# Gate logits of the linear attention: one stacked single-pass product instead of a float32 product

## What is computed

```python
IN_COLS = 2 * GLA_KW + 2 * GLA_VW + 2 * GATE_RANK + 3 * CONV_W     # GATE_RANK = 16, GLA_KW = 512
q, k, v, g, lf, lb, cb, cc, cx = split_proj(hx @ w_in[i])
la_f = heads(jax.nn.log_sigmoid((lf @ w_gf + b_gf).astype(jnp.float32)) / GATE_NORM, GLA_DK)
la_b = heads(jax.nn.log_sigmoid((lb @ w_gb + b_gb).astype(jnp.float32)) / GATE_NORM, GLA_DK)
```

## Time and profile before

| | |
|---|---|
| median of 3 runs | 2288.86 us (2288.14 to 2289.62) |
| span of the profiled execution | 2285.8 us |
| TensorE busy | 2266.4 us, 99% |
| TensorE weight loads busy | 1864.5 us, 82% |
| VectorE busy | 1556.3 us, 68% |
| ScalarE busy | 1109.7 us, 49% |
| GpSimd busy | 223.5 us, 10% |
| mean granted TensorE clock | 0.997 of 2.4 GHz |

### The profile page before, as it was taken

One profiled execution on the slowest core, in us unless ns is written; L12 is line 12 of the kernel. 1 busy time (PEld: TensorE's weight loads), 2 busy tenths in 40 slices (PEclk: granted clock), 3 DMA queues, 4 the chain that ended last, 5 costly groups with the idle time before them and its releaser, 6 DMA issues.

```text
span 2285.8 us, 28964 instructions
## 1 busy us (share of the span) xinstructions
PE 2266.4 (99%) x10345; PEld 1864.5 (82%) x10345; DVE 1556.3 (68%) x1869; ACT 1109.7 (49%) x1531; POOL 223.5 (10%) x361
## 2 busy tenths in 40 slices
PE   9999999999999999999999999999999999999998
PEld 7888888888888888888878877787888888888886
DVE  7886778778867877887767664556555545555556
ACT  6446455555545545545463463545444344444444
POOL 0121001111111111110011000000210011100110
PEclk9999999999999999999999999999999999999999
DMA  8983679978888888886677664564665666656663
GB/s 311 331 272 97 206 235 320 317 267 293 275 281 287 273 301 269 272 280 215 220 242 245 209 203 129 186 220 158 210 203 194 207 207 198 207 185 201 195 195 126
DMA packets 250005, 528.12 MB, mean 231 GB/s; under 512 B 22144, under 2 KB 22544, under 8 KB 248592
## 3 DMA queue, kind: packets, MB, share of 16 engines
q1 hardware_dynamic: 214256, 405.32, 54.2%
q0 software_dynamic: 33664, 116.17, 14.8%
q10 hardware_dynamic: 1952, 4.85, 0.6%
HBM read 517.87 MB, written 4.21 MB: 228 GB/s over the span
## 4 chain that ended last, share of the span: by engine, by line
PE 97%; DVE 1%; ACT 1%; DMA 0%; issue 0%; SPq 0%; ACTq 0%; DVEq 0%; POOLq 0%
PE acc L1798 30%; PE acc L1807 29%; PE acc L1802 29%; PE tp L1869 2%; PE m L1880 1%; PE acc L1820 0%; PE acc L1825 0%; PE acc L1830 0%; PE tp L2206 0%; PE tp L2224 0%; PE tp L2218 0%; PE acc L2000 0%; PE tp L2131 0%; PE acc L1853 0%; PE acc L1851 0%
## 5 line engine op out<-in xcount | busy, mean ns | idle before, releaser
L1090 DVE TENSOR_TENSOR wlo<-wring,whi 128x1024 fp32r<-128x1024 f32 x762 | 919.5, 1216 | 562.6 <-ACT whi L565 455.4
L565 ACT ACTIVATE whi<-wring 128x1024 fp32r<-128x1024 f32 (+1 forms) x510 | 532.1, 1047 | 720.4 <-PE acc L1807 719.3
L1798 PE MATMUL acc<-whi,xhi 128*128 128x512 f32 x2056 | 558.5, 393 | 0.1
L1802 PE MATMUL acc<-whi,xlo 128*128 128x512 f32 x2056 | 550.0, 389 | 0.0
L1807 PE MATMUL acc<-wlo,xhi 128*128 128x512 f32 x2056 | 549.9, 389 | 0.0
L1802 PEld LDWEIGHTS acc<-whi,xlo 128*128 128x128 f32 x2056 | 386.0, 188 | 81.1
L1807 PEld LDWEIGHTS acc<-wlo,xhi 128*128 128x128 f32 x2056 | 386.0, 188 | 80.7
L1798 PEld LDWEIGHTS acc<-whi,xhi 128*128 128x128 f32 x2056 | 381.2, 188 | 86.3 <-issue 9.0
L575 ACT ACTIVATE whi<-wring 128x1024 fp32r<-128x1024 f32 x266 | 280.8, 1059 | 319.8 <-PE acc L1807 318.1
L1120 DVE SCALAR_TENSOR_TENSOR macc<-mring,csil,macc 128x512 f32<-128x512 f32 x480 | 344.0, 747 | 29.3 <-DMA mring<-w_mod 23.0
L460 POOL DMA_DIRECT2D mring<-w_mod x192 | 138.9, 724 | 1047.4 <-DVE macc L1120 998.9
(11 more groups left out here) (277 smaller groups left out, 1313.7 us busy)
## 6 DMA issues: line engine op xcount, KB each, us to landing
wring<-w_up SPq DMA_DIRECT2D x216, 512.0 KB, 4.7
wring<-w_down SPq DMA_DIRECT2D x216, 512.0 KB, 5.1
mring<-w_mod POOLq DMA_DIRECT2D x192, 512.0 KB, 5.3
wring<-w_in SPq DMA_DIRECT2D x184, 512.0 KB, 5.2
wring<-w_gate SPq DMA_DIRECT2D x88, 512.0 KB, 4.3
wring<-w_out SPq DMA_DIRECT2D x64, 512.0 KB, 4.9
tmpT<-blk POOLq DMA_DIRECT2D x128, 32.0 KB, 3.4
gbig<-ctx_in POOLq DMA_DIRECT2D x2, 1024.0 KB, 8.1
```

Source lines behind the costliest of these rows:

```text
L565: act.activation(whi[:, piece_slot(c, piece), 0:half], wring[:, g4, piece * half:(piece + 1) * half], ACT.Copy).then_inc(hi_done, 1)
L1090: dve.tensor_tensor(wlo[:, h4, 0:half], wring[:, g4, piece * half:(piece + 1) * half], whi[:, h4, 0:half].bitcast(F32), ALU.subtract).then ...
L1798: pe.matmul(acc[:, 2 * pair + t, :], hi[:, tile, t * P:(t + 1) * P], whi[:, h4, w], start=(tile == starts), stop=False)
L1802: pe.matmul(acc[:, 2 * pair + t, :], lo[:, tile, t * P:(t + 1) * P], whi[:, h4, w], start=False, stop=False)
```

## The change

The gate product takes the same split into rounded value and remainder, but the parts stand below each other along the contraction, in one 128-row product of type float32r. Rows 0 to 31 of `lrankT` are the rounded rank values, rows 32 to 63 their remainders, rows 64 to 95 the rounded values again, and rows 96 to 127 ones. `wg` has the rounded gate matrix in the first two row groups and its remainder in the third; in row 96 the rounded bias, in row 97 its remainder, and zeros below.

To get the rank values three times, the rank block's weights are written three times side by side (`round_rank`, `remainder_rank`, 96 columns), so its product gives 96 rows. ScalarE copies all 96, and VectorE puts the remainder into rows 32 to 63 (`rank_split`). `wg` is put together once: GpSimd loads the matrix, the bias and zeros in ten DMAs into two scratch areas, `wg_raw` and `wg_rest`, ScalarE rounds `wg_raw` to `wg` and VectorE combines rows 64 to 127 with `wg_rest`. That is the new step `stack_gates`, at (cc0, 3) ahead of `z`, and the gate product waits for it (`wg_stacked`).

```diff
@@ -41,6 +41,7 @@
 RANK2 = 32
+RANK_ROWS = 3 * RANK2
 OFF_Q, OFF_K, OFF_V, OFF_G, OFF_L, OFF_CB, OFF_CC, OFF_CX = 0, 512, 1024, 2048, 3072, 3104, 4128, 5152
@@ -144,6 +145,7 @@
         ones = small[:, 14, 0:1]
+        gate_sign = small[:, 14, 1:2]
         blk = sb("blk", [P, T, NB])
@@ -183,15 +185,17 @@
             states = sb("states", [P, 2, GH, DV], scope=ph)
-            wg = sb("wg", [P, 2, GH * DK], scope=ph)
+            wg = sb("wg", [P, 2, GH * DK], F32R, scope=ph)
             gbig = sb("gbig", [P, 2 * D], scope=ph)
             gk = sb("gk", [P, T, GH * DK], scope=ph)
-            lrankT = sb("lrankT", [P, S], scope=ph)
+            lrankT = sb("lrankT", [P, S], F32R, scope=ph)
             epos = sb("epos", [P, 2, S], scope=ph)
             orstd = sb("orstd", [P, T, GH], scope=ph)
+        wg_raw = silg[:, 0, :].rearrange("p (d c) -> p d c", d=2)
+        wg_rest = silg[:, 1, :].rearrange("p (d c) -> p d c", d=2)
         u_g = gbig[:, :].rearrange("p (t d) -> p t d", t=T)
@@ -241,7 +245,8 @@
         ctx_in_s = sem("ctx_in_s")
-        wg_in = sem("wg_in")
+        wg_in, wg_rounded, wg_stacked, rank_split, sign_set = (
+            sem(n) for n in ("wg_in", "wg_rounded", "wg_stacked", "rank_split", "sign_set"))
         spill_s = sem("spill_s")
@@ -336,10 +341,10 @@
         BESIDE[1].update({
-            ("cc0", 3): (("z", 0, 0, 0),), ("cx0", 0): (("z", 0, 0, 1),),
+            ("cc0", 3): (("stack_gates", 0, 0, 0), ("z", 0, 0, 0)), ("cx0", 0): (("z", 0, 0, 1),),
             ("cx0", 1): (("z", 0, 1, 0),), ("cx0", 2): (("z", 0, 1, 1),),
             ("cx0", 3): (("suffix", 0, 0, 0), ("suffix", 0, 0, 1)), ("cb0", 0): (("suffix", 0, 1, 0), ("suffix", 0, 1, 1)),
             ("cb0", 1): (("ctx_state", 0, 0, 0),), ("cb0", 2): (("ctx_state", 0, 1, 0),),
@@ -370,6 +375,15 @@
         MOVES = 16 * 16
+        def rank_piece(slot, piece):
+            src = wring[:, slot, piece * 4 * RANK2:(piece + 1) * 4 * RANK2].rearrange("p (k n) -> p k n", k=4)
+            return src.unsqueeze(2).broadcast_to([P, 4, 3, RANK2])
+        def thrice(dst, slot):
+            return dst[:, slot, 0:4 * RANK_ROWS].rearrange("p (k c n) -> p k c n", k=4, c=3)
         block = ctx.enter_context(nc.Block())
@@ -518,9 +532,23 @@
             pool.wait_ge(h_added, H_MLP)
-            pool.memset(lrankT[RANK2:RANK2 + 1, :], 1.0).then_inc(pool_set, 1)
+            pool.wait_ge(pool_set, 1)
+            pool.memset(gate_sign[2 * RANK2:P, :], -1.0).then_inc(sign_set, 1)
+            pool.wait_ge(sign_set, 1)
+            pool.memset(gate_sign[RANK_ROWS:RANK_ROWS + 1, :], 1.0).then_inc(sign_set, 1)
+            pool.wait_ge(sign_set, 2)
+            pool.memset(lrankT[RANK_ROWS:P, :].bitcast(F32), 1.0).then_inc(pool_set, 1)
             pool.wait_ge(in_set, IN_SET[0]["v1"])
-            pool.dma_start(wg[:, :, :], gates_w).then_inc(wg_in, 16)
+            bias, zeros = gates_w[RANK2:RANK2 + 1], gates_w[RANK2 + 1:RANK2 + 31]
+            for copy in range(3):
+                pool.dma_start(wg_raw[RANK2 * copy:RANK2 * (copy + 1)], gates_w[0:RANK2]).then_inc(wg_in, 16)
+            for row in range(2):
+                pool.dma_start(wg_raw[RANK_ROWS + row:RANK_ROWS + row + 1], bias).then_inc(wg_in, 16)
+            pool.dma_start(wg_raw[RANK_ROWS + 2:P], zeros).then_inc(wg_in, 16)
+            pool.dma_start(wg_rest[2 * RANK2:RANK_ROWS], gates_w[0:RANK2]).then_inc(wg_in, 16)
+            pool.dma_start(wg_rest[RANK_ROWS:RANK_ROWS + 1], zeros[0:1]).then_inc(wg_in, 16)
+            pool.dma_start(wg_rest[RANK_ROWS + 1:RANK_ROWS + 2], bias).then_inc(wg_in, 16)
+            pool.dma_start(wg_rest[RANK_ROWS + 2:P], zeros).then_inc(wg_in, 16)
             with c.loop(pool, 4, m=8, ma=16) as i:
@@ -565,6 +593,15 @@
                     c.add("g")
+            def round_rank():
+                g4 = c.slot("g", WSLOTS)
+                for piece in range(SPLIT):
+                    act.wait_ge(piece_landed[g4][piece], c.landed("g", WSLOTS))
+                    act.wait_ge(piece_multiplied, c.at("g", piece + 1, SPLIT))
+                    act.activation(thrice(whi, piece_slot(c, piece)), rank_piece(g4, piece), ACT.Copy).then_inc(hi_done, 1)
+                c.add("g")
@@ -876,7 +913,7 @@
                     act.wait_ge(pool_set, 2)
-                    act.activation(lrankT[0:RANK2, :], acc[0:RANK2, 2 * pair, 0:S], ACT.Copy).then_inc(in_set, 1)
+                    act.activation(lrankT[0:RANK_ROWS, :], acc[0:RANK_ROWS, 2 * pair, 0:S], ACT.Copy).then_inc(in_set, 1)
                 elif name == "k":
@@ -922,6 +959,9 @@
                     act.activation(kdec[:, a, b], tp[:, c.slot("q", 2), :], ACT.Exp).then_inc(kdec_exp, 1)
+                elif kind == "stack_gates":
+                    act.wait_ge(wg_in, 16 * 10)
+                    act.activation(wg[:, :, :], wg_raw, ACT.Copy).then_inc(wg_rounded, 1)
                 elif kind == "conv_operand":
@@ -955,10 +995,10 @@
                             round_groups(1)
-                        elif kg < 2:
+                        elif kg < 2 or following != "l":
                             round_groups(1)
                         else:
-                            round_groups(1, 8 * RANK2 if following == "l" else KG * NB)
+                            round_rank()
                         if last:
@@ -1090,6 +1130,16 @@
                     c.add("g")
+            def remainder_rank():
+                g4 = c.slot("g", WSLOTS)
+                for piece in range(SPLIT):
+                    h4 = piece_slot(c, piece)
+                    dve.wait_ge(hi_done, c.at("g", piece + 1, SPLIT))
+                    dve.tensor_tensor(thrice(wlo, h4), rank_piece(g4, piece), thrice(whi, h4).bitcast(F32),
+                                      ALU.subtract).then_inc(lo_done, 1)
+                c.add("g")
@@ -1423,8 +1473,12 @@
-            def store_block(name, pair):
+            def store_block(name, pair, p):
                 src = acc[:, 2 * pair:2 * pair + 2, :]
+                if name == "l":
+                    dve.wait_ge(in_set, IN_SET[p]["l"])
+                    dve.tensor_tensor(lrankT[RANK2:2 * RANK2, :], acc[RANK2:2 * RANK2, 2 * pair, 0:S],
+                                      lrankT[RANK2:2 * RANK2, :].bitcast(F32), ALU.subtract).then_inc(rank_split, 1)
                 if name in ("cx0", "cx1"):
@@ -1506,6 +1560,13 @@
                             dve.copy_predicated(sc[:, d, t, :], keep[d], m1[:, (2 * d + t) * P:(2 * d + t + 1) * P]).then_inc(gsc_kept, 1)
+                elif kind == "stack_gates":
+                    rows = slice(2 * RANK2, P)
+                    dve.wait_ge(sign_set, 2)
+                    dve.wait_ge(wg_rounded, 1)
+                    dve.scalar_tensor_tensor(wg[rows, :, :], wg[rows, :, :].bitcast(F32), gate_sign[rows, :],
+                                             wg_rest[rows, :, :], ALU.mult, ALU.add).then_inc(wg_stacked, 1)
                 elif kind == "beyond":
@@ -1561,10 +1622,13 @@
                         last = kg == (1 if name == "l" else 3)
-                        remainders(1, 8 * RANK2 if name != "l" and kg >= 2 and following == "l" else KG * NB)
+                        if name != "l" and kg >= 2 and following == "l":
+                            remainder_rank()
+                        else:
+                            remainders(1)
                         if last:
                             wait_block(2)
-                            store_block(name, (48 + n) % 2)
+                            store_block(name, (48 + n) % 2, p)
                         for st in BESIDE[p].get((name, kg), ()):
@@ -1769,13 +1833,13 @@
-                dst = acc[0:RANK2, 2 * pair, 0:S]
+                dst = acc[0:RANK_ROWS, 2 * pair, 0:S]
                 for piece in range(SPLIT):
                         tile = half * 8 + piece * 4 + k
-                        w = slice(k * RANK2, (k + 1) * RANK2)
+                        w = slice(k * RANK_ROWS, (k + 1) * RANK_ROWS)
                         pe.matmul(dst, whi[:, h4, w], hi[:, tile, :], start=(tile == 0), stop=False)
@@ -2124,11 +2188,11 @@
-                    pe.wait_ge(in_set, IN_SET[p]["l"])
+                    pe.wait_ge(rank_split, p + 1)
                     pe.wait_ge(pool_set, 2)
-                    pe.wait_ge(wg_in, 16)
+                    pe.wait_ge(wg_stacked, 1)
                     pe.wait_ge(tp_free, c.at("q", 1))
-                    pe.matmul(tp[:, q, :], lrankT[0:RANK2 + 1, a * P:(a + 1) * P], wg[0:RANK2 + 1, b, :], start=True, stop=True).then_inc(tp_ready, 1)
+                    pe.matmul(tp[:, q, :], lrankT[:, a * P:(a + 1) * P], wg[:, b, :], start=True, stop=True).then_inc(tp_ready, 1)
                     c.add("q")
```

## The result

The changed kernel takes 2297.95 us (median of 5 runs, 2296.25 to 2300.08), the kernel before, on the same chip, 2288.86: 9.1 us more, ratio 1.0036 with a 95% interval of 1.0024 to 1.0049. The forecast was 2293.5, with a range to 2297.6: right in its sign and about half the size. The median lies 0.35 us above the range; the ratio stands for 8.2 us more, 2297.1, which lies inside it. The profiled span is 2294.5 us, 8.7 more than before.

What follows compares the result with a forecast made beforehand. TensorE was taken as the bound, busy 2266.4 of 2285.8 us. The terms + 6.2 - 2.05 - 1.85 + 2.3 gave + 4.6 us: a profiled span of 2290.4, a median of 2293.5, range 2289.2 to 2297.6.

Steps and rivals of the forecast that it cites:

- Gate products: On TensorE, each of eight becomes one single-pass product, 1.04 us less each, 8.3 us in all; waits ahead taken as 0.
- Rank block: On TensorE, 96 products load 96 columns instead of 32; cost taken as 0, at most 4.7 us.
- The wait for the stack: Ahead of the first gate product TensorE waits for `stack_gates`: at least 4.4 us, 6.2 us with VectorE's lateness.
- GpSimd's queue: Ten DMAs issue the first `mring` load 4.4 us later; landing in 5.2 us, it makes VectorE 1.8 us late.
- rival (b): Late transfer of the `mring` loads: 4.5 us instead of 1.8, + 2.7, total 2296.2; chance 0.15.
- The cap: ScalarE's rounds of 6.27 us limit the gain ahead of the suffixes: 2.05 us in the first four products, 1.85 in the second.
- Rival (d): The stack is not waited for: 2280.6 with all 8.3 us, or 2285.0 with ScalarE's rounds as they are; chance 0.06.
- The clock: After the stall at the first gate product TensorE runs at 1.2 GHz for a while: 2.3 us lost, bounds 0 and 3.4.
- the second four: Tokens' four gate products in the last pass: 25.7 us to the suffix instead of 27.57, a gain of 1.85 us.
- (a): Clean stall: `mring` loads come as before and the clock holds, + 0.5, total 2289.4; chance 0.17.
- (c): In the rank block, loads of 96 columns are not overlapped: + 4.7 us, total 2298.2; chance 0.07.
- (e): The gate product still goes as two long records, its operand only relabelled: total 2297.4; chance 0.05.

Runs made afterwards that it cites:

- e_two: Changed kernel with two DMAs of 128 rows in place of its ten small ones, output not the reference's; 2296.26 us, ratio 1.0030 to the kernel before.
- e_pool: Changed kernel with the first two loads of `mring` issued ahead of the ten DMAs; 2293.81 us, ratio 1.0020 to the kernel before.
- e_early: Changed kernel with `stack_gates` one group earlier, at (cc0, 2); 2293.25 us, ratio 1.0014 to the kernel before.
- e_fastz: Kernel before with single-pass gate products and nothing else, remainders of the split left out; 2287.30 us, ratio 0.9990.
- e_both: Changed kernel with `stack_gates` at (cc0, 2) and the first two `mring` loads ahead of the ten DMAs; 2288.86 us, ratio 0.9997 to the kernel before.
- e_rank: Kernel before with only the rank block widened, 96 columns instead of 32; 2289.67 us against 2289.47, ratio 1.0001.
- e_all: e_both with the suffix products one group later and the first three context states moved back; 2288.79 us, ratio 0.9994 to the kernel before.
- e_fastz_free: e_fastz with suffixes and context states one group later and VectorE's modulation steps ahead of the steps beside them; 2286.67 us, ratio 0.9987 to the kernel before.
- e_ctl: Kernel before with only suffixes and context states one group later and VectorE's modulation steps ahead of the steps beside them; 2290.54 us against 2289.45, ratio 1.0003.

## Why the prediction was half right

**Gate products: right.** 1.04 us each was said, 1.07 measured (6.733 - 5.667), so the waits ahead of them cost nothing. They follow each other at 5.66 to 5.67 us.

**Rank block: a small miss.** 0 was taken, 0.2 us in each pass measured. Its 48 products take 1305.09 to 1310.74, 0.118 us each, against 0.114. The record of a load of 96 columns is 162 ns, longer than the 118 from one product to the next, and all but those 4 ns of it is hidden. The Trainium skill (TensorE: Matmul & The Clock Gate, LDWEIGHTS) gives columns divided by 1.2 in ns, 80 ns for 96 columns. By that the load fits under the product, which agrees but for the 4 ns; the record itself is twice the page's figure.

**The wait for the stack: mechanism and floor right.** The forecast was 4.41 us plus the lateness of VectorE. With the lateness read where the modulation steps end and the pair of remainders starts (before: 1133.80 - 1113.65 = 20.15):

| | remainders start | late by | 27.80 + 4.41 + late | z0 |
|---|---|---|---|---|
| changed | 24.87 | 4.72 | 36.93 | 36.89 |
| e_two | 22.24 | 2.09 | 34.30 | 34.27 |
| e_pool | | 0 | 32.21 | 32.53 |

The table also answers for the wait of 1.91 us and the halved clock behind it: they lie inside the same delay, as the prediction had it for its upper end, and nothing is left for them in the row of the changed kernel, 36.93 against 36.89.

**GpSimd's queue: the step that failed.** It has two parts. The later issue was sized right: 4.15 us later, counted from A, against the 4.4 of the text. The landing was not: "After the change the first two meet a less loaded queue: I take 5.2 us" and "a second one just in time". It was 7.67 us, and VectorE waited 0.83 us more for the second load. The queue ahead was not less loaded: the ten carry 768 KB where one carried 512. Whether the bytes set the time is not shown: with 768 KB ahead it is 7.67 (7.68 in e_early), no more than with 512, and only 1024 KB stand out, 8.68 in e_two. Nor did the DMA engines make it up. The stretch 1128 to 1132 us, the last two columns DMA share and GB/s, of the changed kernel:

```profile
1128.00:1132.00 4.00, 4.00 (x19) 3.34 (x18) 0.00 (x0) 1.90 (x2) 0.58 (x1) 1.00 1.06 241
```

and of the one before:

```profile
1128.00:1132.00 4.00, 4.00 (x19) 3.34 (x18) 1.01 (x2) 2.12 (x2) 0.00 (x0) 1.00 1.03 398
```

They are as busy and move 241 GB/s instead of 398. Why is open. So 4.7 us came instead of 1.8, +2.9. That is rival (b), given only 0.15 because "the queue ahead is emptier"; the 7.8 us of the earlier trace rows was the better witness.

**The cap: right, for this kernel.** 24.8 and 25.7 us to the suffixes; measured 24.79 (e_early, no loss of clock) and 25.66. (The terms of the first, 19.44 + 4.58 + 0.69, add up to 24.7; the text has rounded up.) But the 2.05 us are there only because z0 is late. e_fastz and e_both show 0.75 without a stall. Rival (d) counted on them without a stall and came to 2285.0; it should have said 1.3 us more.

**The clock: size of the first loss right, second missed.** z0 to z1 takes 7.84 us against 5.75 in e_early: 2.1, where 2.3 was said. That is partly luck: TensorE went on 2.7 us later than forecast, and the clock also fell later (granted 1.00 from 1145 to 1147 and 0.73 from there to 1149, against 1145.4 in the forecast), so that about 4.4 us of work stood at the low clock where the forecast had 4.6. A fall before that, behind the wait of 1.91 us, was not forecast. The sum had none behind the suffix waits, though it named idle times "of 1 to 2 us" there. The second was 2.83 us, and the granted clock fell to 1.2 GHz: 22.95 instead of 21.28, +1.67. The Trainium skill (TensorE: Matmul & The Clock Gate, What's actually happening) says that the throttled state is the default and activity releases it; the runs agree as far as every drop stands behind a wait, and don't show from which wait on.

**Sum.** 2.88 (z0 later than forecast, the late loads) + 1.67 (second loss) + 0.20 (rank block) - 0.32 (first loss and the second four) = 4.43, the difference between +4.6 forecast and +9.04 measured. So nearly all of the miss is two terms: the landing of the loads, sized too small, and the second loss of clock, put at nothing.

**The rivals.** (a) needed loads as early as before and a full clock, and had neither. (b) came for the loads, without the second loss. (c) is ruled out by e_rank, (e) by records of 0.39 us. (d) became true only when the stack was moved and GpSimd's order changed, and then the gain went first into the suffix's wait (e_both), then into the reduction's (e_all). The chances of (c) and (d), which the range leaves out, are 0.13 together, not 0.15.

## What to carry to other kernels

A gain on the bounding engine comes in only as far as the chains beside it have slack: here ScalarE's chain left 0.7 us of the 4.2 that the context's four products could give, and each wait removed brought up the next one behind it, at the suffix, the reduction, the stack, the convolution. Find the next latest arrival before counting a gain, and put preparation a group ahead of its use on every engine that takes part. Count a queue's issues; here a load behind ten small DMAs came late by the issues and landed no faster for their being small. A wait of two or three microseconds on TensorE can be paid nearly twice (3.13 us and 2.9 us of lost clock behind it in e_both), and can also cost nothing more than itself.

## What the runs showed of the hardware

- A product of a 33-row operand among products of 128 rows costs 0.61 us (6.07 - 5.46, two half groups), one of 128 rows 0.21 (5.67 - 5.46), with the same 512 columns. The Trainium skill (TensorEngine Tiling (Array Packing), Key Properties) says "Changing tiling mode (not just tile) drains the TensorE"; the rows of e_fastz fit that, with 0.35 us of idle ahead of the load and 0.24 behind, but no run shows that the 33 rows were a change of mode. Single pass with 33 rows gains 0.67 us a product (e_fastz_free against e_ctl), with 128 rows 1.07: 0.4 comes of filling the rows.
- The small DMAs cost GpSimd 0.48 to 0.52 us each in the changed kernel, whatever their size (4 to 128 KB), and took 5.8 to 6.2 us to land in the median, 4 KB as long as 128.
- The length of a wait alone doesn't say whether the clock falls. 2.83 us ahead of the tokens' suffix was followed by 1.2 GHz in the changed kernel and not in e_both. Ahead of the context's suffix, 1.84 us in the changed kernel was not, the same wait of 1.9 us in e_early was (s to z4 140.78 instead of 139.04). What else decides is open.

In e_both, around the wait ahead of the tokens' suffix (the suffix starts at 1339.16), the third column from the right is again the granted clock:

```profile
1336.00:1338.00 2.00, 0.33 (x2) 0.00 (x0) 0.00 (x0) 1.97 (x3) 0.00 (x0) 1.00 0.77 265
1338.00:1340.00 2.00, 0.84 (x2) 0.49 (x3) 1.55 (x3) 2.00 (x3) 0.00 (x0) 1.00 0.92 265
1340.00:1344.00 4.00, 4.00 (x17) 2.85 (x16) 4.00 (x6) 2.56 (x4) 0.72 (x1) 1.00 0.60 185
```
